# Differential attention with scores two tiles ahead and three probability buffers per map, the combination first in VectorE's order

## The reference, cut to what matters

```
# differential attention: 4 heads, two maps (m = 0, 1) of 64 columns each, value width 128, causal, ALiBi
sc = einsum('bqhmd,bkhmd->bhmqk', q, k) * 64**-0.5 - slope[h] * (qpos - kpos)      # masked where kpos > qpos
p = softmax(sc)
a = p[map 0] - lam * p[map 1]
do = rms_norm(a @ v, diff_norm)

# memory attention, after the mixer's output projection
q = rms_norm((h @ w_q).reshape(.., 4 heads, 256), q_norm)
k = rms_norm(mem_n @ w_k, k_norm);  v = mem_n @ w_v           # 256 memory rows, 4 heads of 256
o = softmax(q @ k * 256**-0.5) @ v
```

## Time and profile before

| | us |
|---|---|
| median of 3 runs | 2165.74 (2164.62 to 2169.53) |
| profiled execution, its own time | 2164.66 |
| its span, first to last instruction | 2162.8 |
| TensorE busy | 2102.0 (97%) |
| GpSimd busy | 1396.4 (65%) |
| VectorE busy | 775.2 (36%) |
| ScalarE busy | 501.8 (23%) |

### The profile page before, as it was taken

One profiled execution on the slowest core, in us unless ns is written; L12 is line 12 of the kernel. 1 busy time (PEld: TensorE's weight loads), 2 busy tenths in 40 slices (PEclk: granted clock), 3 DMA queues, 4 the chain that ended last, 5 costly groups with the idle time before them and its releaser, 6 DMA issues.

```text
span 2162.8 us, 29025 instructions
## 1 busy us (share of the span) xinstructions
PE 2102.0 (97%) x9198; PEld 1672.5 (77%) x9198; DVE 775.2 (36%) x1242; ACT 501.8 (23%) x911; POOL 1396.4 (65%) x1372
## 2 busy tenths in 40 slices
PE   7999999999999999989999999999899999999997
PEld 5878866678888888767888887877667778888885
DVE  4123344443320122282223126344765452221024
ACT  2023243331210121141110012134652421110011
POOL 5643333367777777667777779655667357777675
PEclk8999999999999999999999999999999999999998
DMA  7311111122222223222222224222222112222221
GB/s 247 114 58 39 49 49 49 49 78 97 97 97 97 97 96 105 92 78 88 97 97 98 97 97 165 91 74 69 88 78 98 59 59 97 97 97 97 97 97 58
DMA packets 55682, 193.84 MB, mean 90 GB/s; under 512 B 6303, under 2 KB 8607, under 8 KB 55236
## 3 DMA queue, kind: packets, MB, share of 16 engines
q1 hardware_dynamic: 51500, 184.05, 25.2%
q10 hardware_dynamic: 4120, 8.95, 1.2%
HBM read 190.85 MB, written 5.27 MB: 91 GB/s over the span
## 4 chain that ended last, share of the span: by engine, by line
PE 90%; DVE 5%; ACT 3%; issue 1%; DMA 0%; DVEq 0%; POOL 0%; SPq 0%; ACTq 0%; POOLq 0%
PE acc L274 26%; PE acc L276 26%; PE acc L275 26%; PE st L320 2%; PE ob L669 1%; PE sc L654 1%; PE ob L482 1%; DVE ssum L398 1%; PE sc L495 1%; PE sc L1500 1%; PE sc L497 1%; PE tp L662 1%; DVE arena L1619 0%; PE tp L528 0%; PE st L617 0%
## 5 line engine op out<-in xcount | busy, mean ns | idle before, releaser
L1705 POOL TENSOR_TENSOR w_lo<-w_raw,w_hi 128x512 fp32r<-128x512 f32 x684 | 927.4, 1356 | 57.1
L1703 POOL TENSOR_SCALAR w_hi<-w_raw 128x512 fp32r<-128x512 f32 x684 | 471.1, 689 | 689.1 <-PE acc L276 657.4
L274 PE MATMUL acc<-h_hi,w_hi 128*128 128x512 f32 x1936 | 779.6, 403 | 20.1 <-DVE h_lo L1838 8.6
L276 PE MATMUL acc<-h_hi,w_lo 128*128 128x512 f32 x1936 | 756.4, 391 | 0.0
L275 PE MATMUL acc<-h_lo,w_hi 128*128 128x512 f32 x1936 | 756.1, 391 | 0.0
L274 PEld LDWEIGHTS acc<-h_hi,w_hi 128*128 128x128 f32 x1936 | 365.5, 189 | 112.1 <-issue 26.1
L275 PEld LDWEIGHTS acc<-h_lo,w_hi 128*128 128x128 f32 x1936 | 365.7, 189 | 84.7 <-issue 10.6
L276 PEld LDWEIGHTS acc<-h_hi,w_lo 128*128 128x128 f32 x1936 | 365.1, 189 | 77.3
L274 PE MATMUL acc<-hid_hi,w_hi 128*128 128x512 f32 x608 | 236.9, 390 | 0.1
L276 PE MATMUL acc<-hid_hi,w_lo 128*128 128x512 f32 x608 | 236.6, 389 | 0.0
L275 PE MATMUL acc<-hid_lo,w_hi 128*128 128x512 f32 x608 | 236.5, 389 | 0.0
(11 more groups left out here) (255 smaller groups left out, 1774.4 us busy)
## 6 DMA issues: line engine op xcount, KB each, us to landing
w_raw<-in_wstream SPq DMA_DIRECT2D x342, 512.0 KB, 3.5
x<-in_xT SPq DMA_DIRECT2D x4, 512.0 KB, 6.4
bias_skew<-bias_rows ACTq DMA_DIRECT2D x4, 512.0 KB, 7.4
out_y<-x SPq DMA_DIRECT2D x8, 256.0 KB, 2.2
arena<-bias_skew ACTq DMA_DIRECT2D x4, 257.5 KB, 3.8
bias_skew<-bias_rows ACTq DMA_DIRECT2D x4, 256.0 KB, 8.0
arena<-in_memT ACTq DMA_DIRECT2D x1, 1024.0 KB, 8.4
arena<-in_decay ACTq DMA_DIRECT2D x1, 1024.0 KB, 11.8
```

The lines of the kernel that those rows point to most:

```text
L274: nc.tensor.matmul(dst, w_hi[:, slot, k, :], xh[:, k, :], start=first, stop=False)
L276: done = nc.tensor.matmul(dst, w_lo[:, slot, k, :], xh[:, k, :], start=False, stop=last)
L1703: nc.gpsimd.tensor_scalar(w_hi[:, slot, ks, :], w_raw[:, raw, ks, :], 1.0, 0.0, ALU.mult, ALU.add).then_inc(w_rounded, 1)
L1705: nc.gpsimd.tensor_tensor(w_lo[:, slot, ks, :], w_raw[:, raw, ks, :], w_hi[:, slot, ks, :].bitcast(F32), ALU.subtract).then_inc(w_split, 1)
```

## The change

In the differential attention a third probability buffer is added for each map, in two blocks of the retention's decay table, which is not read any more. TensorE's scores, ScalarE's exponentials and VectorE's row maxima run two tiles ahead of the transposition instead of one. VectorE's tile t becomes: `combine` of t, `inverse` of t + 1, `d_scored_dve` of t + 2, then the copy and the tail as before; the low half of retention head 3 moves ahead of the first of all these. On ScalarE `inv` runs one tile ahead, and two squares move: `o_sq` ahead of the exponentials, `k_sq` ahead of `copy_pt`. In the memory attention query unit 2 moves ahead of `qstat(0)` on TensorE, and its scaling ahead of `q_norm(0)` on VectorE.

```diff
-        p_d = [[a2(28), a2(29)], [a2(32), a2(31)]]
+        p_d = [[a2(28), a2(29), a2(dt0)], [a2(32), a2(31), a2(dt0 + 1)]]
@@ d_scored_dve
-            dve.wait_ge(turned, TILES0["diff"] + 4 * h + qt - 1)
-            dve.wait_ge(s("d_a"), counted(4 * h + qt - 1))
-            nc.vector.tensor_tensor_reduce(p_d[m][(e // 2) % 2][:, 0:w], ...
+            dve.wait_ge(turned, TILES0["diff"] + 4 * h + qt - 2)
+            dve.wait_ge(s("d_a"), counted(4 * h + qt - 2))
+            nc.vector.tensor_tensor_reduce(p_d[m][(e // 2) % 3][:, 0:w], ...
@@ diff_pe
             score(0, 0, 0)
             score(0, 0, 1)
             d_v_turn_pe(pe, 3)
+            score(0, 1, 0)
+            score(0, 1, 1)
             for tile in range(4 * QT):
                 h, qt = divmod(tile, QT)
-                if tile < 4 * QT - 1:
-                    score((tile + 1) // QT, (tile + 1) % QT, 0)
-                    score((tile + 1) // QT, (tile + 1) % QT, 1)
+                if tile < 4 * QT - 2:
+                    score((tile + 2) // QT, (tile + 2) % QT, 0)
+                    score((tile + 2) // QT, (tile + 2) % QT, 1)
                 if tile in DIFF_STAT:
                     diff_stat_pe(pe, tile)
                 mem_unit(pe, tile)
@@ diff_act
             ret_high_act(act, 3)
+            exp(0, 1, 0)
+            exp(0, 1, 1)
+            inv(0, 0)
             for tile in range(4 * QT):
                 h, qt = divmod(tile, QT)
-                inv(h, qt)
                 if tile < 4 * QT - 1:
-                    exp((tile + 1) // QT, (tile + 1) % QT, 0)
-                    exp((tile + 1) // QT, (tile + 1) % QT, 1)
+                    inv((tile + 1) // QT, (tile + 1) % QT)
+                if h and qt == 1:
+                    o_sq(h - 1)
+                if tile < 4 * QT - 2:
+                    exp((tile + 2) // QT, (tile + 2) % QT, 0)
+                    exp((tile + 2) // QT, (tile + 2) % QT, 1)
                 if tile in DIFF_STAT:
                     stat_of(tile)
+                if tile + 1 in DIFF_STAT and DIFF_STAT[tile + 1][:2] == "mk":
+                    k_sq(int(DIFF_STAT[tile + 1][2]))
                 if h and qt == 0:
                     o_copy(h - 1)
                 if tile in (11, 15):
                     v_copy((tile - 11) // 4)
                 copy_pt(h, qt)
-                if tile + 1 in DIFF_STAT and DIFF_STAT[tile + 1][:2] == "mk":
-                    k_sq(int(DIFF_STAT[tile + 1][2]))
-                if h and qt == 1:
-                    o_sq(h - 1)
@@ diff_dve
+            ret_low_dve(dve, 3)
+            d_scored_dve(dve, 0, 1, 0)
+            d_scored_dve(dve, 0, 1, 1)
+            inverse(0, 0)
             for tile in range(4 * QT):
                 h, qt = divmod(tile, QT)
-                inverse(h, qt)
+                combine(h, qt)
                 if tile < 4 * QT - 1:
-                    d_scored_dve(dve, (tile + 1) // QT, (tile + 1) % QT, 0)
-                    d_scored_dve(dve, (tile + 1) // QT, (tile + 1) % QT, 1)
-                combine(h, qt)
-                if tile == 0:
-                    ret_low_dve(dve, 3)
+                    inverse((tile + 1) // QT, (tile + 1) % QT)
+                if tile < 4 * QT - 2:
+                    d_scored_dve(dve, (tile + 2) // QT, (tile + 2) % QT, 0)
+                    d_scored_dve(dve, (tile + 2) // QT, (tile + 2) % QT, 1)
@@ mem_pe
+            out1(pe, "mem_q", 2, 0, h1_hi, h1_lo)
             qstat(0)
-            out1(pe, "mem_q", 2, 0, h1_hi, h1_lo)
             score(0, 0)
             score(0, 1)
@@ mem_dve
             scaled1(dve, "mem_q", 1, a2(13))
+            scaled1(dve, "mem_q", 2, a2(14))
             q_norm(0)
-            scaled1(dve, "mem_q", 2, a2(14))
             top(0, 0)
```

More of the change, by code:

```diff
@@ L1045, in d_scored_dve @@
                 dve.wait_ge(s("d_vtr"), 4)
-            dve.wait_ge(turned, TILES0["diff"] + 4 * h + qt - 1)
-            dve.wait_ge(s("d_a"), counted(4 * h + qt - 1))
-            nc.vector.tensor_tensor_reduce(p_d[m][(e // 2) % 2][:, 0:w], sc[m][:, 0:w], alibi_s[:, h, SEQ - w:SEQ], 1.0,
+            dve.wait_ge(turned, TILES0["diff"] + 4 * h + qt - 2)
+            dve.wait_ge(s("d_a"), counted(4 * h + qt - 2))
+            nc.vector.tensor_tensor_reduce(p_d[m][(e // 2) % 3][:, 0:w], sc[m][:, 0:w], alibi_s[:, h, SEQ - w:SEQ], 1.0,
                                            -LOWEST, ALU.add, ALU.min, mx[:, e % 8:e % 8 + 1]).then_inc(row_max, 1)
@@ L1285, in turn @@
                 for kt in range(qt + 1):
-                    m = nc.tensor.transpose(tp[e % 2][:, kt * P:(kt + 1) * P], p_d[0][e % 2][:, kt * P:(kt + 1) * P], ident)
+                    m = nc.tensor.transpose(tp[e % 2][:, kt * P:(kt + 1) * P], p_d[0][e % 3][:, kt * P:(kt + 1) * P], ident)
                 m.then_inc(turned, 1)
@@ L1317, in exp @@
                 act.wait_ge(row_max, WIDE0["diff"] + e + 1)
-                p = p_d[m][(e // 2) % 2][:, 0:w]
+                p = p_d[m][(e // 2) % 3][:, 0:w]
                 nc.scalar.activation(p, p, ACT.Exp, bias=mx[:, e % 8:e % 8 + 1], scale=-1.0,
@@ L1324, in inv @@
                 act.wait_ge(row_inv, TILES0["diff"] + e // 2 + 1)
-                p0 = p_d[0][(e // 2) % 2][:, 0:(qt + 1) * P]
+                p0 = p_d[0][(e // 2) % 3][:, 0:(qt + 1) * P]
                 nc.scalar.activation(p0, p0, ACT.Identity, scale=rl[:, e % 8:e % 8 + 1]).then_inc(s("d_p0"), 1)
@@ L1410, in combine @@
                 k, w = e % 8, (qt + 1) * P
-                p0, p1 = p_d[0][(e // 2) % 2][:, 0:w], p_d[1][(e // 2) % 2][:, 0:w]
+                p0, p1 = p_d[0][(e // 2) % 3][:, 0:w], p_d[1][(e // 2) % 3][:, 0:w]
                 dve.wait_ge(s("d_p0"), e // 2 + 1)
```

## The result

| | before | changed |
|---|---|---|
| median, us | 2165.36 (6 runs, 2163.39 to 2169.53) | 2176.64 (6 runs, 2173.81 to 2182.34) |
| ratio to before, 95% interval | | 1.0053 [1.0036, 1.007] |
| profiled execution's own time, us | 2164.66 | 2180.3 |
| mean granted clock of TensorE | 0.991 | 0.987 |

The change costs 11.3 us; the forecast was 12 us (2177.7). The profiled execution of the changed kernel is 3.7 us above its median, so its 15.6 us over the profile of before are more than the change costs, and I account for them by landmarks. The first scores of the differential stage start 2.45 us later than before; nothing ahead of them was changed, so I count this as a difference between two executions. From those scores to head 3's value product the stage takes 101.57 us in place of 91.81 (+9.8). The memory attention's start adds 4.0, and 0.5 us come back behind it.

A forecast was written before the change was run, and what follows sets the result against it. TensorE, busy 97%, was taken as the bound, with the VectorE/ScalarE statistics loop close behind. Stage 4.7, memory attention 2.6 and clock 4.6 gave +11.9 us on 2164.66, 2176.6; median 1.1 higher, 2177.7 us, range 2168 to 2184.

The forecast's parts named there:

- the sum: Whole kernel: stage 4.7, memory attention 2.6 and clock 4.6 us, together 11.9 us slower.
- The hole at the start: Start of differential stage: tile 2's scores wait at least 5.1 us for VectorE to read tile 1's scores.
- The tiles: Later differential stage: waits move from combination to statistics' shared bank, 11.2 us in place of 11.6; statistics loop 7.7 us.
- unit 12: Differential stage: TensorE waits 0.9 us because ScalarE copies this unit's bank behind two later exponentials.
- The memory attention: Memory attention's start: the chain from statistic to scores loses its cover, taking 7.1 us; costs 2.6 us.
- The lower bound: Memory attention: both norms at the lowest of their rows, 0.75 us each, beside an idle GpSimd; costs 2.6 us.
- The clock behind the two holes: After the differential stage's start and the memory attention's bare chain: half speed, 2.3 us each, bounds 0 and 3.
- The clock elsewhere: Rest of the differential stage: no clock loss counted, since waits up to 1.5 us had left it at full.
- rival 1: Differential stage: the lead works and later waits vanish; +0.7 us, 2166.4 us, no change; chance 0.12.
- rival 2: Clock holds behind one or both holes: +7.3 to +9.6 us, 2173 to 2175.3 us; chance 0.18.
- rival 3: Whole kernel faster: listed stage waits all go, full clock in both holes; -3.9 us, 2161.8 us; chance 0.03.
- Rival 4: Differential stage: the loop stretches more, combinations starting as GpSimd splits; +3 us, 2180.7 us; chance 0.10.

The follow-up runs named there:

- e2: Changed kernel with the memory attention in its old order, only the differential attention's edits kept: 2170.82 us, 6.1 us above before.
- e4: Whole changed kernel plus five spare 512-column matmuls in each of TensorE's two long waits: 2171.64 us, 6.9 us above before.
- e1: Kernel before with only the memory attention's edit, query unit 2 and its scaling moved ahead: 2168.81 us, 4.1 us above before.
- e3: As e2, but TensorE does tile 0's memory unit ahead of tile 2's scores: 2169.02 us, 4.3 us above before.
- e5: As e3, but in VectorE's tile the combination stands behind the reciprocals and the maxima of two tiles on: 2169.16 us, 3.3 us above before.
- e6: As e3, but ScalarE does the statistic and the next tile's square ahead of exponentials two tiles on: 2166.38 us, 0.5 us above before.
- e9: e6 plus earlier maxima and exponentials of tile 1, tile 0's reciprocals ahead of retention head 3's product, its low half later: 2163.32 us, 2.2 us below before.
- e10: Kernel before, scores one tile ahead, with only ScalarE's statistic moved ahead of the next tile's exponentials: 2163.26 us, 2.3 us below before.
- e11: e9 plus two spare matmuls ahead of tile 0's transposition and two ahead of statistic mk0: 2161.9 us, 2.9 us below before.

## Why the prediction was right

The direction, the size and the main mechanism were right: a hole behind VectorE's queue, a bare chain in the memory attention, and half clock behind both. That the sum came within 1 us of the 11.3 is in part luck: it had 7.3 us for the order and 4.6 for the clock, and the runs showed about 4 to 6 and about 7.

- **The hole at the start**: 5.1 us expected, 4.85 measured, with the maximum as releaser and the low half just ahead of it. Line 1102 took 0.69 us where I had taken 0.75.
- **The tiles**: "11.2 us in place of 11.6" was too high. The waits behind the hole add up to 9.0 us. mk0 (3.0 for 2.4), tile 7 (1.3 for 0.8) and tile 11 (1.4 for 0.7) were under-rated; do0 (0.3 for 1.5), do1 (0.8 for 2.6), mk3 (none for 0.4) and mk2 (0.4 for 1.0) over-rated. The value product (1.2 for 0.9) was under-rated, unit 12 (0.4 for 0.9) over-rated. The loop from mk2 to mk3 was 7.50 us for the 7.7 worked out, but 1.0 of it is the norms behind GpSimd's split; with the same order and no such meeting it was 6.53 (e2), so the working, which took durations of before, was over 1 us too long, and the near hit is luck. The reading that the waits move from the combination to the statistics held: in e2 and e4 from 5.4 to none at the combination (1.5 expected) and from 3.8 to 6.5 at the statistics (7 expected); in the changed kernel's profile in half that size, 2.7 and 4.7. At full clock the stage lost 3.7 us in the changed kernel and 2.5 to 2.9 in e2 and e4; the sum had 4.7.
- **The memory attention**: 2.6 us expected, 2.4 measured in three profiles. The two norms took 1.42 us beside an idle GpSimd, where I had 1.5; the chain 6.9 us for 7.1. The lower bound was the right one to take.
- **The clock behind the two holes**: 2.3 us each expected; 2.9 and 1.6 measured, and 4.4 us came back against before in e4.
- **The clock elsewhere**: the step that failed was to price the clock behind the two holes alone, because "in the differential stage the waits, up to 1.5 us, left it at full". It fell twice more in the profile of the changed kernel, for 3.2 us, once behind the 3.0 us at mk0 (forecast at 2.4, and not counted as a hole) and once behind 1.3 us at tile 7 and 0.4 at mk2. That is why the stage in the profile lost 9.8 us and not my 7.0 (4.7 and 2.3). e2 had only one of these two falls, and its median was 6.1 us above before.
- **The rivals**: that the lead works (rival 1) is excluded by e2, that the clock holds (rival 2) by e1 and e4, and rival 3 with both. Rival 4's mechanism, VectorE's operations meeting GpSimd's split, is in the changed kernel's profile and e3's but not in e2's or e4's; it cost about 1 us and not 3 (95.5 us at full clock for e2's 94.3).

## What to carry to other kernels

A longer lead makes an engine wait earlier in its list for work that another engine has not reached: before moving a step forward, ask what of the other engines stands ahead of its input, and what the step now blocks. Where several chains share engines, first do the work that somebody waits for: putting the statistic ahead of the exponentials made the stage as short with one tile of lead as with two. One profile is one meeting of engines as well as one order: the loop of 7.50 us had 1.0 us in it that the same order did not have in the next kernel. A unit of independent work between a statistic and its user is cover; moved ahead of the statistic it takes away one wait of 1.5 us and bares a chain of 7.

## What the runs showed of the hardware

The granted clock fell to half behind waits of 1.4 to 2.1 us in this stretch of small score and transposition matmuls (e3, e5, e6, e9), and around 1.3 us at a transposition and 0.3 to 0.9 at the statistic after it (tile 7 in the changed kernel and e3, tile 3 in e5), where the profile of before had a wait of 1.46 us and kept it. It fell at mk0 in e1 and e10, behind a wait of 1.4 us, with the very order on TensorE that kept it in before. So whether it falls is in part chance of the execution, and one profile is not enough to price it. Each fall cost 1.4 to 3.4 us. The Trainium skill, page "TensorE: Matmul & The Clock Gate", section "What's actually happening", says that the monitor runs free of the kernel, so that the moment of a change depends on where the activity lands. By that rule one order can lose here and not there, and the traces of before, e1 and e10 agree. With five spare matmuls in each of its two long waits the changed kernel kept full clock behind both (e4). With some 3.4 us of them in all (eight passes of 0.43 us) the profile of e11 has full clock through the whole stage, but that is its shortest execution, and e9's shortest ones have the same mean clock without them.

The two 256-column norms of mk2 on VectorE took 0.88 us beside an idle GpSimd (e2, e4, e5) and 1.77 where GpSimd had begun its two-input subtraction (line 1714) 0.2 us before them (changed kernel, e3). A 512-column combination took 0.79 us where it began before that subtraction (e2) and 1.70 where it began 0.1 us after it (changed kernel).
